# Residual rows loaded early into two weight slots, and three of eight residual adds moved from VectorE to GpSimd

## What is computed

```python
x = x + g_m * rms_norm(y, norm_mix_post[l])            # called x2 in the kernel
h = rms_norm(x, norm_ffn_pre[l]) * (1.0 + sc_f) + sh_f
y = hier_moe(h, ...)                                    # sum over two experts of gate * expert row
x = x + g_f * rms_norm(y, norm_ffn_post[l])             # the last stage
return x
```

## Time and profile before

| | us |
|---|---|
| median of 3 runs (1474.76 to 1475.43) | 1475.35 |
| the profiled execution | 1474.47 |
| its span, first to last instruction | 1472.6 |
| busy in the span: PE / DVE / ACT / POOL | 1343.0 / 628.6 / 398.8 / 121.4 |
| HBM traffic | 282.54 MB read, 27.82 MB written |
| expert stage's last matmul ends about | 1426.1 |
| first d_y load issued | 1431.55 |
| last VectorE instruction starts | 1468.02 |

### The profile page before, as it was taken

How to read it: one execution, slowest core, us unless ns; L and a number is a source line. 1 busy time by engine, 2 the same in 40 slices (tenths; PEclk the granted TensorE clock), 3 DMA queues, 4 the chain that set the end, 5 groups by cost and what they waited for, 6 DMA issues and landing times.

```text
span 1472.6 us, 17016 instructions
## 1 busy us (share of the span) xinstructions
PE 1343.0 (91%) x6333; PEld 677.6 (46%) x6333; DVE 628.6 (43%) x1387; ACT 398.8 (27%) x888; POOL 121.4 (8%) x149
## 2 busy tenths in 40 slices
PE   4899999999998798999899984999899999989965
PEld 3654444464565444445455552454344444434422
DVE  3516347520234666666646548232322322222317
ACT  4233311112566565555523320000000000000004
POOL 0000000001000700000010001011111111111110
PEclk9899999999998899999999986999999999999997
DMA  9811335430001600000053477899999999999969
GB/s 334 188 43 57 114 115 198 143 115 0 1 1 45 77 1 1 1 0 1 0 228 130 162 306 283 324 391 391 405 402 399 405 401 394 397 412 393 406 254 398
DMA packets 90527, 306.29 MB, mean 208 GB/s; under 512 B 28317, under 2 KB 32573, under 8 KB 82121
## 3 DMA queue, kind: packets, MB, share of 16 engines
q1 hardware_dynamic: 83160, 288.34, 52.5%
q0 software_dynamic: 6736, 16.81, 3.2%
q10 hardware_dynamic: 544, 0.02, 0.0%
HBM read 282.54 MB, written 27.82 MB: 211 GB/s over the span
## 4 chain that ended last, share of the span: by engine, by line
PE 37%; DMA 9%; SPq 5%; DVE 4%; issue 2%; ACT 1%; PEldq 0%; PEld 0%; DVEq 0%; ACTq 0%; POOLq 0%
DMA arena<-expert_w 7%; PE ps L1732 7%; PE ps L1640 7%; PE ps L1771 7%; PE ps L1719 6%; SPq L717 4%; PE ps L1519 2%; PE ps L1538 2%; PE ps L1558 2%; PE ps L1709 2%; PE ps L1592 1%; DMA arena<-d_y 1%; DMA arena<-d_xn,arena 1%; ACT arena L1156 1%; PE ps L1576 0%
## 5 line engine op out<-in xcount | busy, mean ns | idle before, releaser
L1369 PE MATMUL ps<-arena 128*128 128x512 f32 x512 | 222.0, 593 | 0.0
L1732 PE MATMUL ps<-arena 128*32 128x256 f32 (+1 forms) x1408 | 190.2, 490 | 14.2 <-DMA arena<-expert_w 12.4
L1771 PE MATMUL ps<-arena 128*32 128x256 f32 (+2 forms) x832 | 152.7, 498 | 3.4 <-DMA arena<-expert_w 1.7
L1369 PEld LDWEIGHTS ps<-arena 128*128 128x128 f32 x512 | 96.6, 190 | 117.8 <-issue 117.7
L1380 PE MATMUL ps<-arena 128*128 128x512 f32 (+1 forms) x384 | 145.3, 537 | 1.4 <-DVE arena L1875 1.4
L1732 PEld LDWEIGHTS ps<-arena 128*32 128x32 f32 (+1 forms) x1408 | 72.0, 124 | 118.2 <-issue 102.2
L1719 PE MATMUL ps<-arena 128*128 128x512 f32 x256 | 113.7, 601 | 2.8 <-DVE arena L2284 2.8
L1156 ACT ACTIVATE arena<-arena 128x640 f32<-128x640 f32 (+7 forms) x128 | 92.7, 726 | 61.2 <-DVE arena L2089 61.2
L1380 PEld LDWEIGHTS ps<-arena 128*128 128x128 f32 x384 | 73.3, 193 | 66.5 <-issue 58.8
L2089 DVE CUSTOM_DVE_ANT_0 arena<-ps,arena 128x640 f32<-128x640 f32 (+7 forms) x128 | 84.5, 705 | 40.6 <-PE ps L1519 38.5
L1538 PE MATMUL ps<-arena 128*128 128x128 f32 x528 | 82.0, 288 | 20.7 <-ACT arena L1156 12.8
(11 more groups left out here) (379 smaller groups left out, 1363.4 us busy)
## 6 DMA issues: line engine op xcount, KB each, us to landing
arena<-expert_w SPq DMA_DIRECT2D x96, 2048.0 KB, 33.9
arena<-ada_w SPq DMA_DIRECT2D x12, 2048.0 KB, 9.2
arena<-x SPq DMA_DIRECT2D x16, 512.0 KB, 5.3
arena<-w_in SPq DMA_DIRECT2D x4, 2048.0 KB, 10.8
d_xn<-arena SPq DMA_DIRECT2D x8, 1024.0 KB, 4.1
arena<-d_y SPq DMA_DIRECT2D x16, 512.0 KB, 10.7
arena<-w_out SPq DMA_DIRECT2D x2, 2048.0 KB, 10.7
d_x<-arena SPq DMA_DIRECT2D x8, 512.0 KB, 2.9
```

Source lines behind the costliest of these rows:

```text
L1369: last = nc.tensor.matmul(b, w(k), hT[:, k, 512 * c:512 * c + 512], start=(k == 0), stop=(k == KT - 1))
L1732: last = nc.tensor.matmul(ps[width * j:width * j + width, 2 if width == 64 else 3, 0:span], xgT[s][:, k, lo:lo + width], w_up[slots[n]][:, ...
L1771: last = nc.tensor.matmul(dst, hid_T[s][:, at_:at_ + width], w_down[slot][:, k, span * j:span * j + span], start=(k == 0), stop=(k == 3))
```

## The change

The residual rows no longer go to the slots of the last block, but to those of w1 and w3 of block NQ - 3 = 30 (`X2_USES`), which are free earlier. SP issues all eight residual loads directly behind the last weight load, ahead of the loop of overflow blocks, each four behind the wait that their slot is read out. The overflow blocks all use one fixed set of three slots instead of two sets in turn, and `load_over` waits accordingly. GpSimd adds the residual of tiles 1, 3 and 5 at the end of its own program and counts `g_done_pool`; VectorE skips these three adds, and SP's stores wait for the one count or the other.

```diff
-OVER_SLOT = [[SLOT_OF[USES[len(LOADS) - NS + 3 * s + j]] for j in range(3)] for s in range(2)]
+X2_USES = [(1, NQ - 3), (3, NQ - 3)]
+X2_SLOT = [SLOT_OF[u] for u in X2_USES]
+OVER_SLOT = [SLOT_OF[u] for u in ((2, NQ - 4), (1, NQ - 2), (3, NQ - 2))]
...
-        x2_slots = [SLOT_OF[(n, NQ - 1)] for n in (1, 3)]
+        ON_POOL = (1, 3, 5)
...
+            for t in range(NT):
+                if t % 4 == 0:
+                    slot_free(X2_USES[t // 4])
+                sp.dma_start(x2_back[t], d_x2[t * P:(t + 1) * P, :]).then_inc(x2_in[t], 16)
             sp.wait_ge(table_ready, 1)
...
-            sp.wait_ge(up_done, NQ)
-            def load_residual(t):
-                sp.dma_start(x2_back[t], d_x2[t * P:(t + 1) * P, :]).then_inc(x2_in[t], 16)
-
-            for t in range(2):
-                load_residual(t)
             sp.wait_ge(stage_f, 3)
...
                     sp.dma_start(y[t], d_y[(k * NT + t) * P:(k * NT + t + 1) * P, :]).then_inc(tile_in[t], 16)
-                if t >= 2:
-                    load_residual(t)
             for t in range(NT):
-                sp.wait_ge(g_done, t + 1)
+                if t in ON_POOL:
+                    sp.wait_ge(g_done_pool, ON_POOL.index(t) + 1)
+                else:
+                    sp.wait_ge(g_done, t + 1 - sum(u < t for u in ON_POOL))
                 sp.dma_start(out[t * P:(t + 1) * P, :], y1[t]).then_inc(out_stored, 16)
...
+            for t in ON_POOL:
+                pool.wait_ge(g_normed, t + 1)
+                pool.wait_ge(x2_in[t], 16)
+                nc.gpsimd.tensor_tensor(y1[t], y1[t], x2_back[t], ALU.add).then_inc(g_done_pool, 1)
...
                 V.scalar_tensor_tensor(a, total, rs, gf_row, ALU.mult, ALU.mult).then_inc(g_normed, 1)
+                if t in ON_POOL:
+                    continue
                 dve.wait_ge(g_normed, t + 1)
                 dve.wait_ge(x2_in[t], 16)
                 V.tensor_tensor(a, a, x2_back[t], ALU.add).then_inc(g_done, 1)
```

More of the change, by code:

```diff
@@ L130 @@
     FILLS[u] = 16 * fills[SLOT_OF[u]]
-OVER_SLOT = [[SLOT_OF[USES[len(LOADS) - NS + 3 * s + j]] for j in range(3)] for s in range(2)]
-OVER_FILLS = [[16 * fills[j] for j in slots] for slots in OVER_SLOT]
+X2_USES = [(1, NQ - 3), (3, NQ - 3)]
+X2_SLOT = [SLOT_OF[u] for u in X2_USES]
+OVER_SLOT = [SLOT_OF[u] for u in ((2, NQ - 4), (1, NQ - 2), (3, NQ - 2))]
+OVER_FILLS = [16 * fills[j] for j in OVER_SLOT]
 STORES = [0, 0]
@@ L457, in build @@
         BY_PRODUCT = (1, 3, 5, 7)
-        x2_slots = [SLOT_OF[(n, NQ - 1)] for n in (1, 3)]
-        x2_back = [view(SLOT[x2_slots[t // 4]] + D * (t % 4), D) for t in range(NT)]
-        y_slots = [SLOT[j] for j in range(NS) if j not in x2_slots]
+        ON_POOL = (1, 3, 5)
+        x2_back = [view(SLOT[X2_SLOT[t // 4]] + D * (t % 4), D) for t in range(NT)]
+        y_slots = [SLOT[j] for j in range(NS) if j not in X2_SLOT]
         y1 = [view(y_slots[i // 4] + D * (i % 4), D) for i in range(NG)]
@@ L495, in build @@
         mod_hop = sem("mod_hop")
-        stage_f = sem("stage_f")
+        stage_f, g_done_pool = sem("stage_f"), sem("g_done_pool")
         idx_seen, store_seen = sem("idx_seen"), sem("store_seen")
@@ L779, in load_over @@
                 e = sp.value_load(block_tab[0:1, bass.ds(PER * i + s + 1, 1)], min_val=0, max_val=NE - 1)
-                sp.wait_ge(down_done, PER * i + NQ - 3 + s)
+                sp.wait_ge(up_done, PER * i + NQ + s)
                 sp.sem_inc(idx_seen, 1)
-                sp.wait_ge(up_done, PER * i + NQ - 1 + s)
+                load_weight(OVER_SLOT[0], 1, e)
+                load_weight(OVER_SLOT[1], 3, e)
+                sp.wait_ge(down_done, PER * i + NQ + s)
                 sp.sem_inc(idx_seen, 1)
[L784 to L788, removed]
+                load_weight(OVER_SLOT[2], 2, e)
+            for t in range(NT):
+                if t % 4 == 0:
+                    slot_free(X2_USES[t // 4])
+                sp.dma_start(x2_back[t], d_x2[t * P:(t + 1) * P, :]).then_inc(x2_in[t], 16)
             sp.wait_ge(table_ready, 1)
@@ L1799, in over_block @@
             def over_block(i, s):
-                q, slots, b = PER * i + NQ + s, OVER_SLOT[s % 2], (NQ + s) % 2
-                nth = PER // 2 * i + s // 2
-                loaded = [16 * nth + 16 + n for n in OVER_FILLS[s % 2]]
+                q, slots, b = PER * i + NQ + s, OVER_SLOT, (NQ + s) % 2
+                loaded = [16 * (PER * i + s) + 16 + n for n in OVER_FILLS]
                 f_turn(q, b, P, PER // 2 * i + (NQ + s) // 2 + 1)
```

## The result

| | before | changed |
|---|---|---|
| median, 8 runs each, us | 1475.07 (1473.56 to 1477.14) | 1478.06 (1475.99 to 1481.48) |
| ratio, 95% interval | | 1.002 (1.0011 to 1.0029) |
| the profiled execution / its span, us | 1474.47 / 1472.6 | 1481.48 / 1479.6 |

The changed kernel is 0.2% slower. On a second chip its ratio was 1.0007 (0.9998 to 1.0016), where no difference can be told, so the size is known only to about 0.1%.

The account below looks back on a forecast made before the run. Tail taken as bound by full DMA engines and, beside them, VectorE (busy 20.65 of 22.00 us). Terms +0.4, 0, 0, -4.0, +5.7 gave +2.1, said as +2.0: median 1477.3 us, own range 1476.2 to 1479.2, with rivals 1471.4 to 1480.2.

Parts of the forecast that it names:

- the likeliest case: Last stage: VectorE and GpSimd take turns as forecast, chance 0.60; own range 1476.2 to 1479.2 us.
- (1), residual loads moved: End of expert stage: eight residual transfers issued behind the last weight load delay the d_y landings, +0.4 us (-0.1 to +1.1).
- (2), the last scatter: Before the first d_y issue: scatter takes 3 to 4 us, nothing added; far end 8.1 us, +4.0.
- The price rule of the late start: Last scatter: nothing up to 4.1 us, then one for one, up to +4.0 at 8.1 us.
- the late start: Start of last stage: residual packets hold up the last scatter and SP's d_y loads; typically 1479.8 us, chance 0.18.
- (3), stores: End of last stage: earlier stores are hidden, the last costs its 2.9 us as now; 0 us.
- (4), three adds off VectorE: VectorE's last-stage chain: three adds and the tile 5 gap go, ScalarE waits come; -4.0 us.
- (5), turns: Last stage: VectorE instructions with two SBUF inputs and GpSimd's three adds wait for each other; +5.7 us (+5.1 to +6.6).
- The mechanism that I gave 0.60: Last stage: GpSimd and VectorE take turns, a whole instruction at a time; chance 0.60.
- The rival in which transfers set the end: Tail: each transfer taken out gives its 1.27 us; -7.6 us, 1467.7 us, chance 0.03.
- Side by side: Last stage: GpSimd's adds do not hinder VectorE; -3.6 us, 1471.7 us, chance 0.17 (wholly or mostly).

Follow-up runs that it names:

- the second profile: The unchanged edit (changed kernel) profiled once more, on a second chip; ratio to the kernel before 1.0007 (0.9998 to 1.0016).
- the first run: Changed kernel with the adds of tiles 1, 3 and 5 back on VectorE, early residual loads kept; ratio to the kernel before 1.0012 (1.0001 to 1.0024).

## Why the prediction was right, and where not

The time was 1478.06 against 1477.3, inside the likeliest case's own range. It is nearer than the change itself was: +2.0 us had been forecast on a median of 1475.35, and +2.99 was measured on one of 1475.07. By its steps:

- *(1), residual loads moved, +0.4.* Measured -0.21 in R, and +0.43 in the second profile, so nothing can be told from +0.4. The last residual tile landed 1440.1 - 1428.4 = 11.7 us after the last weight (11.1 to 11.7 in the five profiles), a little over the 10 to 11.2 of the forecast. SP issued the eight loads over 22 us (1401.5 to 1423.4) and not over 12. The d_y rows were issued later themselves: the fourth landed 7.7 us after the first issue, as in the kernel before (7.75), and 8.2 in the second profile.
- *(2), the last scatter, nothing added.* **The step that failed.** It was put at 3 to 4 us and took 6.3. I had taken the mean DMA share and argued that few engines would still be busy. The mean share was indeed only 0.43 while the scatter ran; my reading is that a scatter lands when its slowest part does, and that part meets the engines that are busy longest. The price rule of the late start held: 6.3 - 4.1 = 2.2, and A grew by 2.20 us. That case had a chance of 0.18, and its sign came true: the first d_y issue at 1438.1, or 1433.8 less the 4.3 us by which this profile is late, is after 1432.5. TensorE's drain, which I had left where it was, moved by 1.4 us as well, beside the scatter.
- *(3), stores, nothing.* The last store took 2.6 us instead of 2.9.
- *(4), three adds off VectorE, -4.0.* The run without them has B 16.64: 20.72 - 16.64 = 4.08.
- *(5), turns, +5.7 (5.1 to 6.6).* Measured 5.06, as 1.78, 1.47 and 1.82 us, where 2.1, 1.8 and 1.8 had been worked out. The smaller share of tiles 3 and 5, where VectorE first stands for the root, is there, but at tile 5 the longer add hides it. Of the 0.6 us too much, 0.3 is GpSimd's add, taken as 2.2 us for 1.99, 1.99 and 2.34. The rest is mostly the start-up of a waiting instruction, put at 0.1 us each without a row that shows it; the scalings ended 1.09 us after the add instead of their own 1.28, which is 0.19. With (4) the net is +0.98, forecast +1.7.

So the time is right partly by luck: errors offset. The turns were 0.6 us too dear, (1) by 0.6 in this pair of profiles (in the second by nothing), the baseline 0.3 too high, and the start 2.2 us too cheap. The mechanism that I gave 0.60 is shown; the late start, which I had set against it as a rival, is true beside it. The rival in which transfers set the end is refuted by the first run: all six transfers gone from the tail, and B lost 0.90 us, the wait of 0.80 at tile 5 and hardly more. Side by side is refuted by every profile with adds on GpSimd.

What stays open: the large spread of the start of the last stage, 1424.5 to 1431.2 us, which lies mostly in work ahead of the change; and why the packet of instructions starts late with eight residual tiles early and not with six, whose last tile also landed after the branch had ended (1435.6 against 1431.7).

## What to carry to other kernels

An idle stretch of the DMA engines can be filled only up to the point where the next small transfer on the critical path, here the last scatter, meets no queue: count to the landing on the last engine, not to the mean share. An elementwise instruction moved from VectorE to GpSimd is worth its time only while VectorE runs nothing with two SBUF inputs; beside such work it costs most of GpSimd's duration, here 1.7 us for each 1.06 that VectorE itself needed. And a tail whose DMA engines are full can still be bound by one engine's chain: take that chain apart first.

## What the runs showed of the hardware that I had not expected

- GpSimd's add of 128x1024 took 1.99 us for tiles 1 and 3 and 2.34 for tile 5, within 0.01 in every profile that has it. The rows y1 of tile 5 lie in another slot than those of tiles 1 and 3; the residual slots are not the reason, since they differ in the run with the old loads, which has the same three times. Whether y1's slot is the reason no run tells.
- A last scatter behind queued residual loads took about as long as these, up to 6.3 us. That is no ceiling for scatters: the one beside the weight loads, at about 1400 us, took 8.0 to 8.9 us in every profile.
- The longest branch over blocks that don't run took TensorE 3.4 to 3.9 us with two residual tiles early, 3.4 to 3.8 with four to six, and 4.3 to 4.9 with eight, and ended 1.4 us after a 16 KB packet of instructions every time.
- A product of eight 128x512 matmuls took 3.70 us at the 2.4 GHz level, and 5.13 to 6.66 at a mean granted clock of 0.72 to 0.55, after 2.3 to 4.0 us without work; but others after 2.3 to 2.7 us without work took 3.70. What the grant goes by these rows don't settle.
